# Moving the SwiGLU input tiles of a fused decoder layer by 64 and 32 bytes in SBUF

## The chip, the cores and the metric

The kernel runs on one core of one Trainium2 chip. The metric is the device time of one execution in microseconds (us). All tensors are float32 in DRAM, 256 tokens, model width 1024, SwiGLU width 2816.

## What is computed

One layer of a decoder trunk: a SwiGLU block, a gated mixing part (block-sparse attention beside an RWKV-7 recurrence), a second SwiGLU block, and a final RMSNorm.

```python
def swiglu(h, w_gate, w_up, w_down):
    return (jax.nn.silu(h @ w_gate) * (h @ w_up)) @ w_down

x = x + 0.5 * swiglu(rms_norm(x, norm_ffn1), ffn1_gate, ffn1_up, ffn1_down)   # 1024 -> 2816 -> 1024
h = rms_norm(x, norm_mix)
proj = h @ w_in            # q, k, v of attention; r, k, v of RWKV-7; two gates
y_a = moba_attention(...)  # 8 heads of 64
y_b = rwkv7_time_mix(...)  # 8 heads of 64
merged = sigmoid(ga) * (y_a @ proj_a) + sigmoid(gb) * (y_b @ proj_b)
x = x + merged @ w_out
x = x + 0.5 * swiglu(rms_norm(x, norm_ffn2), ffn2_gate, ffn2_up, ffn2_down)
out = rms_norm(x, norm_final)
```

## The kernel before, in words

**Products in three passes.** Every large product is made in float32r from numbers split into a high and a low part. SP loads a piece of a weight matrix (128 partitions x 8 row blocks x 256 columns, 1 MB) into `w_raw` (line 337, the helper `load`), ScalarE copies it to `w_hi` rounded to float32r (line 560), and VectorE subtracts to get `w_lo` (line 933). There are two buffers of each, used in turn. TensorE then runs the helper `three` (lines 1488 to 1490), which for one 128x128 block of weights issues three matmuls into the same place in PSUM:

```python
mm(dst, whi[slot][:, k_, cols], xl, start=start, stop=False)
mm(dst, wlo[slot][:, k_, cols], xh, start=False, stop=False)
return mm(dst, whi[slot][:, k_, cols], xh, start=False, stop=stop)
```

The second argument is the stationary operand, 128 columns of weights, loaded by an instruction of its own (LDWEIGHTS); the third is the moving operand, 256 columns of the input, one for each token. So each matmul needs a new load of weights, and the load for the next matmul runs while the current one streams its input. The first pieces of a stage issue the same three matmuls through another helper (line 1484).

**The stages.** A SwiGLU block has 22 pieces for gate and up (11 of each, in turn; a piece is 8 row blocks x 2 column blocks x 3 = 48 matmuls) and 12 pieces for down (7, 7 and 8 row blocks for each of 4 groups of 256 columns, so 42, 42 and 48 matmuls). That is 1,056 + 528 = 1,584 matmuls of 256 columns in a block, 3,168 in both. The input of gate and up is `hhi_f`/`hlo_f` (1024 x 256, transposed), that of down is `hid_hi_t`/`hid_lo_t` (2816 x 256), which ScalarE and VectorE write piece by piece from `silu` and `prod`. The mixing part in between uses `hhi_m`/`hlo_m`, `yahi`/`yalo`, `ybhi`/`yblo` and `mhi`/`mlo` as inputs in the same way. In one of its products, the attention values, the roles are exchanged: the weights are the moving operand and `hhi_m`/`hlo_m` the stationary one (lines 1764 to 1766).

**Order.** Each engine has its own program, written out by hand; semaphores order them. TensorE waits for `lo_ready` before each piece, ScalarE for the landed load and for `multiplied` of the piece that used the buffer before.

**Where tiles lie.** SBUF tiles are placed one behind the other within a partition, each beginning at the next multiple of 32 bytes. All six weight buffers are 8,192 bytes per partition, so all begin at the same byte modulo 256, which is 128. The blocks inside them are 1,024 bytes apart, and the two column halves 512 bytes, so every block of weights that is loaded begins at 128 modulo 256. Likewise each block of an input tile begins at the same byte modulo 256 as its tile. `pad_f` is a tile that nothing reads or writes. It stands between `h_f` and `hhi_f`, and `hlo_f`, `silu`, `prod`, `hid_hi_t`, `hid_lo_t`, `out_tok`, `x_tok` and a few small ones follow. The tiles of the mixing part use the same space again at another time, from the place of `h_f` on, and are placed without `pad_f`.

| tile | begins at, modulo 256, before | now | input minus weights, modulo 256, before | now |
|---|---|---|---|---|
| `w_hi`, `w_lo`, `w_raw` | 128 | 128 | | |
| `hhi_f`, `hlo_f` (gate, up) | 64 | 0 | 192 | 128 |
| `hid_hi_t`, `hid_lo_t` (down) | 64 | 32 | 192 | 160 |
| `silu`, `prod` | 64 | 0 | | |
| `out_tok`, `x_tok` | 64 | 32 | | |
| `hhi_m`, `yahi`, `ybhi`, `mhi` and their low parts | 64 | 64 | 192 | 192 |
| attention values: moving `w_hi` (128), stationary `hhi_m` (64) | | | 64 (moving minus stationary) | 64 |

Of the kernel before, what the change touches and what calls it, by code (L numbers as in the profile page):

```python
# [30 lines left out]
P = 128  # L31
# [113 lines left out]
def trunk(nc, A, consts, out):  # L145
    bias_dram = nc.dram_tensor("bias_rows", (H, 16, 384), F32, kind="Internal").ap()
    with ExitStack() as ctx:
        def sb(name, shape, dt=F32, scope=ctx):
            return scope.enter_context(nc.sbuf_tensor(name, shape, dt))
# [45 lines left out]

        with ExitStack() as sc:
            h_f = sb("h_f", [P, KD, T], scope=sc)
            sb("pad_f", [P, 48], scope=sc)
            hhi_f = sb("hhi_f", [P, KD, T], F32R, scope=sc)
            hlo_f = sb("hlo_f", [P, KD, T], F32R, scope=sc)  # L200
            silu = sb("silu", [P, 2, T], scope=sc)
            prod = sb("prod", [P, 2, T], scope=sc)
            hid_hi = sb("hid_hi_t", [P, FT, T], F32R, scope=sc)
            hid_lo = sb("hid_lo_t", [P, FT, T], F32R, scope=sc)
            out_tok = sb("out_tok", [P, 2, D], scope=sc)

            x_tok = sb("x_tok", [P, 2, D], scope=sc)
            raw2 = out_tok[:].rearrange("p a d -> p (a d)").rearrange("p (c w) -> p c w", c=KD)
            vec_rows = sb("vec_rows", [NVEC, P], scope=sc)
            rel = sb("rel", [NB, H], scope=sc)  # L210
            tok = sb("tok", [P, 8], scope=sc)
# [1925 lines left out]
```

## Time and profile before

| | us |
|---|---|
| median of 3 runs | 616.38 |
| the three runs | 616.14, 616.38, 626.31 |
| the profiled execution | 616.02 |
| its span, from first to last instruction | 614.2 |
| TensorE busy (matmul) | 604.6, 98% of the span |
| VectorE busy | 421.3, 69% |
| ScalarE busy | 296.7, 48% |
| GpSimd busy | 101.4, 17% |
| granted TensorE clock, mean | 0.999 of full speed |

A matmul is recorded from its start to its modelled end, 0.28 us, and a new one starts every 0.11 to 0.12 us, so that records overlap and "busy" can't tell how fast matmuls follow each other. The distance between the starts of two matmuls is called the spacing here. In a stretch that is full of matmuls it is (length of the stretch + 0.28 us) / number of records in it, since a record counts when any part of it lies in the stretch. For weight loads (0.19 us) it is reckoned from first start to last.

### The profile page before, as it was taken

How to read it: one execution, taken by the hardware profiler on the slowest of the kernel's cores; microseconds unless marked ns; L12 is line 12 of the kernel's file. 1: busy time of each engine (PE TensorE's matmuls, PEld its weight loads, DVE VectorE, ACT ScalarE, POOL GpSimd, SP SyncE). 2: the span in 40 equal slices, each digit the busy share in tenths (PEclk: the TensorE clock that was granted, in tenths of full speed). 3: DMA queues.
4: the chain of work that ended last, by engine and by line, in shares of the span. 5: the costliest groups of instructions: out<-in, count | busy, mean ns of one | idle time of the engine just before them, and what ended most of it. 6: DMA issues, size and time to landing. Idle time of an engine off the chain costs nothing.

```text
span 614.2 us, 14948 instructions
## 1 busy us (share of the span) xinstructions
PE 604.6 (98%) x6454; PEld 588.8 (96%) x6454; DVE 421.3 (69%) x490; ACT 296.7 (48%) x346; POOL 101.4 (17%) x106
## 2 busy tenths in 40 slices
PE   8999999999999999999999999999999999999996
PEld 8999999999999999989889999999999999999996
DVE  5857787765556369989994447878767676665662
ACT  6734665444434284345655546645544444443341
POOL 1116800000113100023205433004000000000130
PEclk9999999999999999999999999999999999999999
DMA  8677666556556335586342233455656566556541
GB/s 282 224 249 226 205 194 186 182 174 196 184 186 204 108 127 168 191 209 170 99 136 75 73 106 106 137 154 190 202 170 186 195 205 205 186 164 210 174 157 68
DMA packets 100734, 105.37 MB, mean 172 GB/s; under 512 B 2276, under 2 KB 98828, under 8 KB 100692
## 3 DMA queue, kind: packets, MB, share of 16 engines
q1 hardware_dynamic: 99380, 101.47, 51.8%
q0 software_dynamic: 1152, 3.02, 2.1%
q8 instruction: 33, 0.54, 0.4%
q10 hardware_dynamic: 160, 0.27, 0.1%
q14 instruction: 9, 0.07, 0.0%
HBM read 103.50 MB, written 1.25 MB: 171 GB/s over the span
## 4 chain that ended last, share of the span: by engine, by line
PE 85%; DVE 8%; DMA 4%; ACT 3%; issue 0%; SPq 0%; ACTq 0%; DVEq 0%
PE two L1488 25%; PE two L1490 23%; PE two L1489 23%; PE two L1484 11%; DVE w_lo L933 4%; DMA w_raw<-in_ffn_up 2%; ACT w_hi L560 2%; DMA w_raw<-in_ffn_gate 1%; DMA x_tok<-in_x 1%; PE two L1820 1%; DVE w_lo L943 0%; PE two L1764 0%; PE two L1766 0%; PE two L1765 0%; ACT w_hi L572 0%
## 5 line engine op out<-in xcount | busy, mean ns | idle before, releaser
L560 ACT ACTIVATE w_hi<-w_raw 128x2048 fp32r<-128x2048 f32 (+1 forms) x86 | 162.5, 1890 | 240.0 <-PE two L1490 196.0
L933 DVE TENSOR_TENSOR w_lo<-w_raw,w_hi 128x2048 fp32r<-128x2048 f32 (+1 forms) x86 | 200.4, 2330 | 83.5 <-ACT w_hi L560 83.1
L1488 PE MATMUL two<-hlo_f,w_hi 128*128 128x256 f32 x640 | 177.3, 277 | 0.9 <-DVE w_lo L933 0.8
L1489 PE MATMUL two<-hhi_f,w_lo 128*128 128x256 f32 x640 | 176.7, 276 | 0.0
L1490 PE MATMUL two<-hhi_f,w_hi 128*128 128x256 f32 x640 | 176.7, 276 | 0.0
L1488 PEld LDWEIGHTS two<-hlo_f,w_hi 128*128 128x128 f32 x640 | 120.1, 188 | 2.0 <-DVE w_lo L933 1.8
L1489 PEld LDWEIGHTS two<-hhi_f,w_lo 128*128 128x128 f32 x640 | 120.2, 188 | 0.0
L1490 PEld LDWEIGHTS two<-hhi_f,w_hi 128*128 128x128 f32 x640 | 120.1, 188 | 0.0
L1488 PE MATMUL two<-hid_lo_t,w_hi 128*128 128x256 f32 x352 | 97.9, 278 | 0.5
L1490 PE MATMUL two<-hid_hi_t,w_hi 128*128 128x256 f32 x352 | 97.3, 276 | 0.0
L1489 PE MATMUL two<-hid_hi_t,w_lo 128*128 128x256 f32 x352 | 97.3, 276 | 0.0
L1488 PE MATMUL two<-hlo_m,w_hi 128*128 128x256 f32 x288 | 82.7, 287 | 0.9 <-DVE w_lo L933 0.9
L1489 PE MATMUL two<-hhi_m,w_lo 128*128 128x256 f32 x288 | 79.8, 277 | 0.0
L1490 PE MATMUL two<-hhi_m,w_hi 128*128 128x256 f32 x288 | 79.8, 277 | 0.0
L1488 PEld LDWEIGHTS two<-hid_lo_t,w_hi 128*128 128x128 f32 x352 | 66.1, 188 | 1.5 <-DVE w_lo L933 1.3
L1490 PEld LDWEIGHTS two<-hid_hi_t,w_hi 128*128 128x128 f32 x352 | 66.2, 188 | 0.0
L1489 PEld LDWEIGHTS two<-hid_hi_t,w_lo 128*128 128x128 f32 x352 | 66.1, 188 | 0.0
L1488 PEld LDWEIGHTS two<-hlo_m,w_hi 128*128 128x128 f32 x288 | 54.2, 188 | 4.0 <-issue 1.7
L1490 PEld LDWEIGHTS two<-hhi_m,w_hi 128*128 128x128 f32 x288 | 54.1, 188 | 0.0
L1489 PEld LDWEIGHTS two<-hhi_m,w_lo 128*128 128x128 f32 x288 | 54.1, 188 | 0.0
L423 POOL TENSOR_TENSOR sqsum<-x 128x512 f32<-128x512 f32 x3 | 3.1, 1042 | 238.7 <-DVE x L1061 210.3
L1004 DVE TENSOR_TENSOR prod<-two,rstd 128x512 f32<-128x512 f32 x22 | 15.2, 692 | 19.8 <-PE two L1490 19.7
(347 smaller groups left out, 983.8 us busy)
## 6 DMA issues: line engine op xcount, KB each, us to landing
w_raw<-in_ffn_up SPq DMA_DIRECT2D x21, 1024.0 KB, 5.3
w_raw<-in_ffn_gate SPq DMA_DIRECT2D x20, 1024.0 KB, 5.3
w_raw<-in_w_in SPq DMA_DIRECT2D x20, 1024.0 KB, 5.1
w_raw<-in_ffn_down SPq DMA_DIRECT2D x16, 896.0 KB, 4.8
w_raw<-in_ffn_down SPq DMA_DIRECT2D x8, 1024.0 KB, 5.2
w_raw<-in_w_out SPq DMA_DIRECT2D x4, 1024.0 KB, 5.1
w_raw<-in_proj_a SPq DMA_DIRECT2D x4, 512.0 KB, 3.6
w_raw<-in_proj_b SPq DMA_DIRECT2D x4, 512.0 KB, 4.1
```

The costliest lines, as they stand in the source:

```text
L423: nc.gpsimd.tensor_tensor(sqsum[:], pair, pair, ALU.mult).then_inc(sg["sq_sum"], 1)
L560: nc.scalar.activation(whi[slot][:, 0:kts], raw[slot][:, 0:kts], ACT.Copy).then_inc(sg["hi_ready"], 1)
L933: nc.vector.tensor_tensor(wlo[slot][:, 0:kts], raw[slot][:, 0:kts], whi[slot][:, 0:kts].bitcast(F32), ALU.subtract).then_inc(sg["lo_ready" ...
L1004: nc.vector.tensor_tensor(prod[:], bank[1][:].rearrange("p (m t) -> p m t", m=2), rstd2, ALU.mult).then_inc(sg["up_taken"], 1)
L1484: return mm(dst, lhsT, rhs, start=start, stop=True, skip_group_check=True)
L1488: mm(dst, whi[slot][:, k_, cols], xl, start=start, stop=False)
L1489: mm(dst, wlo[slot][:, k_, cols], xh, start=False, stop=False)
L1490: return mm(dst, whi[slot][:, k_, cols], xh, start=False, stop=stop)
L1820: return nc.tensor.transpose(dst[:, at:at + C], src, cst[rows, C_SUI:C_SUI + C])
```

## The change

`pad_f` is 32 in place of 48 floats per partition (128 in place of 192 bytes), and a second unused tile of 8 floats (32 bytes) is put between `prod` and `hid_hi_t`. All tiles from `hhi_f` on begin 64 bytes earlier up to `prod`, and 32 bytes earlier from `hid_hi_t` on. No instruction is added, removed or put elsewhere; only addresses differ.

```diff
             h_f = sb("h_f", [P, KD, T], scope=sc)
-            sb("pad_f", [P, 48], scope=sc)
+            sb("pad_f", [P, 32], scope=sc)
             hhi_f = sb("hhi_f", [P, KD, T], F32R, scope=sc)
             hlo_f = sb("hlo_f", [P, KD, T], F32R, scope=sc)
             silu = sb("silu", [P, 2, T], scope=sc)
             prod = sb("prod", [P, 2, T], scope=sc)
+            sb("pad_hid", [P, 8], scope=sc)
             hid_hi = sb("hid_hi_t", [P, FT, T], F32R, scope=sc)
             hid_lo = sb("hid_lo_t", [P, FT, T], F32R, scope=sc)
             out_tok = sb("out_tok", [P, 2, D], scope=sc)
```

## Rows read from the trace of the kernel before

**Rows 1.** The page: busy time by engine, granted clock, and the chain that ended last.
```profile
PE 604.6 (98%) x6454; PEld 588.8 (96%) x6454; DVE 421.3 (69%) x490; ACT 296.7 (48%) x346; POOL 101.4 (17%) x106
...
PEclk9999999999999999999999999999999999999999
...
PE 85%; DVE 8%; DMA 4%; ACT 3%; issue 0%; SPq 0%; ACTq 0%; DVEq 0%
```

**Rows 2.** The page's groups of SwiGLU matmuls: count, busy us, mean ns.
```profile
L1488 PE MATMUL two<-hlo_f,w_hi 128*128 128x256 f32 x640 | 177.3, 277 | 0.9 <-DVE w_lo L933 0.8
...
L1488 PE MATMUL two<-hid_lo_t,w_hi 128*128 128x256 f32 x352 | 97.9, 278 | 0.5
```

**Rows 3.** Busy time by stretch (columns named in the first row), ten stretches full of matmuls.
```profile
core 0: us, PE busy (x) PEld busy (x) DVE busy (x) ACT busy (x) POOL busy (x), PEclk, DMA share, GB/s
19.60:26.60 7.00, 7.00 (x61) 6.95 (x60) 5.51 (x8) 4.83 (x6) 0.00 (x0) 1.00 0.87 291
51.00:131.00 80.00, 80.00 (x708) 80.00 (x707) 61.49 (x56) 41.07 (x38) 23.07 (x25) 1.00 0.62 196
199.70:213.40 13.70, 13.70 (x119) 13.70 (x117) 4.83 (x7) 2.07 (x3) 2.60 (x6) 1.00 0.38 121
217.00:259.00 42.00, 42.00 (x373) 42.00 (x372) 36.43 (x37) 23.01 (x26) 0.00 (x0) 1.00 0.54 176
269.60:274.90 5.30, 5.30 (x47) 5.30 (x47) 3.23 (x3) 0.94 (x2) 2.77 (x6) 1.00 1.02 151
276.50:281.80 5.30, 5.30 (x47) 5.30 (x47) 4.52 (x4) 0.75 (x1) 5.24 (x3) 1.00 0.86 173
391.00:407.00 16.00, 16.00 (x138) 16.00 (x137) 13.36 (x16) 6.45 (x7) 0.00 (x0) 1.00 0.59 198
419.20:436.20 17.00, 17.00 (x145) 16.95 (x144) 14.29 (x16) 11.63 (x13) 4.30 (x2) 1.00 0.60 186
437.50:580.00 142.50, 142.50 (x1260) 142.50 (x1259) 93.95 (x77) 60.99 (x48) 3.38 (x3) 1.00 0.61 194
596.50:606.50 10.00, 10.00 (x87) 10.00 (x87) 3.07 (x3) 3.14 (x4) 0.75 (x1) 1.00 0.00 0
```

**Rows 4.** Timeline in the down product of the second block: TensorE's matmuls around a wait.
```profile
595.34 0.28 PE L1489 MATMUL two<-hid_hi_t,w_lo 128*128 128x256 f32 x1
595.45 0.28 PE L1490 MATMUL two<-hid_hi_t,w_hi 128*128 128x256 f32 x1
595.85 0.39 PE L1488 MATMUL two<-hid_lo_t,w_hi 128*128 128x256 f32 x1
596.08 0.28 PE L1489 MATMUL two<-hid_hi_t,w_lo 128*128 128x256 f32 x1
596.19 0.28 PE L1490 MATMUL two<-hid_hi_t,w_hi 128*128 128x256 f32 x1
```

**Rows 5.** The weight loads at the same place.
```profile
595.85 0.19 PEld L1488 LDWEIGHTS two<-hid_lo_t,w_hi 128*128 128x128 f32 x1 [0.32 <-DVE w_lo L933]
595.96 0.19 PEld L1489 LDWEIGHTS two<-hid_hi_t,w_lo 128*128 128x128 f32 x1
596.08 0.19 PEld L1490 LDWEIGHTS two<-hid_hi_t,w_hi 128*128 128x128 f32 x1
```

**Rows 6.** Timeline: eight weight loads whose matmuls stream two columns each.
```profile
375.59 0.97 PEld L1484 LDWEIGHTS two<-cst,tmp 128*128 128x128 f32 x8
```

**Rows 7.** Timeline of ScalarE and VectorE for one piece of up, second block.
```profile
502.19 1.92 ACT L560 ACTIVATE w_hi<-w_raw 128x2048 fp32r<-128x2048 f32 x1 [3.00 <-PE two L1490]
504.14 2.29 DVE L933 TENSOR_TENSOR w_lo<-w_raw,w_hi 128x2048 fp32r<-128x2048 f32 x1 [0.54 <-ACT w_hi L560]
507.63 1.92 ACT L560 ACTIVATE w_hi<-w_raw 128x2048 fp32r<-128x2048 f32 x1 [3.00 <-PE two L1490]
```

**Rows 8.** The same two engines for one piece of down, second block.
```profile
575.69 1.71 ACT L560 ACTIVATE w_hi<-w_raw 128x1792 fp32r<-128x1792 f32 x1 [3.73 <-PE two L1490]
577.43 3.00 DVE L933 TENSOR_TENSOR w_lo<-w_raw,w_hi 128x1792 fp32r<-128x1792 f32 x1
```

**Rows 9.** What the weight loads waited for: us in total, times, longest.
```profile
PEld two L1488 <- DVE w_lo L933: 4.2, 7, 1.1
```

## The prediction

> **What bounds the kernel now.** I read the page first. TensorE is busy 98% of the span at full granted clock, and the chain that ended last is TensorE for 85% of its length [rows 1]. VectorE (69%) and ScalarE (48%) come next, so the time is how fast matmuls follow each other. The counts say whose matmuls they are: 3 x (640 + 352) of the two SwiGLU blocks in the loops [rows 2], to which line 1484 adds 3 x 64, 3,168 together, as the program has it. At 113 to 118 ns each that is about 360 of the 616 us. The change touches only where the inputs of these lie.
>
> "Busy" can't show a spacing, so I took stretches that are full of matmuls of 256 columns and divided. There are two spacings, and hardly anything between them [rows 3]. **The short one**: (142.5 + 0.28) / 1260 = 113.3 ns from 437.5 to 580 us, (80 + 0.28) / 708 = 113.4 from 51 to 131, (42 + 0.28) / 373 = 113.4 in the mixing part from 217 to 259. **The long one**: the stretches from 199.7, 269.6, 276.5, 391 and 596.5 have (13.7 + 5.3 + 5.3 + 16 + 10 + 5 x 0.28) / (119 + 47 + 47 + 138 + 87) = 51.7 / 438 = 118.0 ns. The clock is 1.00 in all of them. Both occur with the same input distance of 192 bytes: the down product has the short one up to 580 and the long one after 596.5. The timeline shows where it went over: TensorE waited for `w_lo`, started again at 595.85, and stayed at the long spacing [rows 4]. So the spacing is a way of running into which the engine falls at a restart and in which it stays until the next one. The reader should see in rows 3 that 142.5 us went by without a change.
>
> What is there besides the 113.3 ns? With matmuls that stream only two columns, eight weight loads follow each other at (0.97 - 0.19) / 7 = 111.4 ns [rows 6]. So loading 128 columns of weights takes nearly the whole of the short spacing, and streaming 256 columns of input beside it adds 1.9 ns in the short way and 6.6 ns in the long way. Those few ns are all that a better place of the tiles can be seen to save, and the rows give no ceiling for what a worse place costs.
>
> **The change part by part.**
> *Gate and up, 192 to 128 bytes (2,112 matmuls), and down, 192 to 160 (1,056).* No row shows either distance. The nearest are on both sides: 192 in nearly all rows, and 64 for the attention values, where the weights are the moving operand; their two stretches (269.6 and 276.5) have (10.6 + 0.56) / 94 = 118.7 ns, the long spacing within the error of such a division, and no worse [rows 3]. 128 and 160 lie between the two. I take the spacing of 192, as the nearer row for 160 and as near as the other for 128, and because it holds for most of the stretches: cost 0. The bounds: from below, all SwiGLU matmuls at the bare weight load. About 250 of them have the long spacing now (61 from 19.6, some 100 of the 145 from 419.2, the rest being the output projection, and 87 from 596.5), and 2,900 the short. That is 2,900 x 1.9 ns + 250 x 6.6 ns = 5.5 + 1.7 = 7.2 us less. The first two loads after the restart are 0.11 us apart, 595.85 and 595.96 [rows 5], which by its rounding allows 110 ns or less: 2,900 x 3.3 + 250 x 8 ns = 11.6 us less as the far end. From above, the nearest row is the long spacing for all: 2,900 x 4.7 ns = 13.6 us more. The farthest row is the restart itself, where a matmul follows the load of its own weights without overlap, 596.08 - 595.85 = 0.23 us [rows 4]: over 300 us more, if loads and streams could not run together at all. As they have run together at both distances on either side, I leave that end out of the range.
>
> *What a faster TensorE would meet.* ScalarE starts `w_hi` when TensorE leaves the buffer (502.19), VectorE has `w_lo` at 504.14 + 2.29 = 506.43, and TensorE turns to that piece about when ScalarE starts the next, 507.63 [rows 7]: 1.2 us to spare, against at most 48 x 3.3 ns = 0.16 us that a piece could become shorter. In the down product 575.69 to 577.43 + 3.00 = 580.43 is 4.74 us, beside 42 x 113.3 ns = 4.76 us of matmuls [rows 8]. Nothing is to spare there when GpSimd slows VectorE, so such a gain would partly turn into waits; they are 4.2 us in seven waits now [rows 9].
>
> *The other tiles.* `silu`, `prod`, `out_tok` and `x_tok` begin at other bytes too. VectorE and ScalarE read and write them, inside the 1.2 us above: cost 0. Without that cover it would be 22 pieces by whatever an instruction got longer, of which no row tells. The transposes of `x_tok` are 16 at the start.
>
> *More or fewer restarts in the long way.* If all SwiGLU matmuls ran at the short spacing, 250 x 4.7 ns = 1.2 us would be saved.
>
> The sum is 0 against the profiled execution, 616.02 us (span 614.2 and 1.8 around it). The median of the runs, 616.38, is 0.4 above. I forecast 616.0. What a measurement of this kernel can tell from no change is about 2%, or 12.3 us here: below 604.1 or above 628.7.
>
> A rule speaks against any effect at all. The Trainium skill, "SBUF — State Buffer", section "Who interferes with whom", gives TensorE two SBUF read ports, one for the moving operand and one for the weight loads, independent of each other, and says that it never waits for anyone. By that rule an address changes nothing and the time is 616.0. The trace agrees only in part: 111.4 ns for a load with little beside it, 113.3 or 118.0 with a stream beside it, so that something is shared or in step between the two.
>
> **The rivals.**
> 1. *The stream stops costing anything.* The 1.9 and 6.6 ns above the bare load are collisions of the two reads, and the new distances avoid them. For it: two spacings for one and the same work look like two orders in which such reads can fall. Against: the short spacing was the same to 0.1 ns in three products, which looks like a fixed price. Time 616.0 - 7.2 = 608.8, with 604.4 as the far end; over 2% only if even the 110 ns is beaten and no wait takes it back.
> 2. *The restarts fall the other way.* At the new distances most restarts end in the long spacing. For it: both stretches at distance 64 are long, and the long one is seen at every kind of input. It needs only that the two restarts ahead of the long loops end so. Time 616.0 + 13.6 = 629.6 if all do. If the one loop of 1,260 does it is 5.9 more, 621.9. The third of the runs shown, 626.31, may have been such a case: 10 us / 4.7 ns is some 2,100 matmuls, but no trace of it exists.
> 3. *The other side: a third, longer spacing.* The order of the two reads at 128 or 160 bytes is a worse one than any seen. The place is every matmul of the loops, the price one more step of the same 4.7 ns: 2,900 x 9.4 + 250 x 4.7 ns = 28.4 us, 644.4. It decides as soon as the mean spacing of SwiGLU matmuls rises by 12.3 us / 3,150 = 3.9 ns, from 113.7 to 117.6 ns, so the long spacing everywhere is just enough. For it: nothing covers a slower matmul in a kernel with TensorE at 98%. Against: distances on both sides have at most 118 to 119 ns.
> 4. *The change doesn't do what it says.* The addresses follow from tile sizes, so only a misreading of what counts (another modulus than 256) could make it so. It ends at 616.0 and belongs to the forecast.
>
> **How the numbers follow.** Forecast, with rival 4: 0.43, between 614.8 and 617.5. Rival 1: 0.18, from 604.4 to 612, of which 0.05 beyond 2%. Rival 2: 0.22, from 618 to 629.6, of which 0.04 above 628.7. Rival 3: 0.17, all of it above. This makes 0.05 faster, 0.21 slower and 0.74 within 2%. The range leaves out half of rival 1's lower part and most of rival 3: 607 to 632. The predicted time is the forecast's own, 616.0.
>
> **What the profile of the changed kernel would show.** Counts as before. For the forecast, 113.3 ns from 437.5 to 580 and from 51 to 131, and the mixing part, whose tiles haven't moved, with 113.4 from 217 to 259 in any case. For rival 1, about 1,280 records in the same 142.5 us and a down product with more than 4.2 us of waits. For rival 2, 118 ns in whole loops and 113 in others. For rival 3, a spacing above 119 ns. If gate and up differ from down, the distance decides and not the restart. I am wrong if the spacing in the loops is neither 113.3 nor 118.0, or if VectorE's instructions on `prod` and `hid_lo_t` get so much longer that the 1.2 us are used up.

## The result, and the profile after

The changed kernel takes 629.97 us (median of 4 executions, 629.09 to 630.40), the kernel before 618.18 in the same comparison (4 executions, 616.14 to 626.31). The ratio is 1.0197, 95% interval 1.0157 to 1.0236: slower, clear of noise, but whether by the 2% that counts as a difference here stays open. Ratios in this document leave out slow executions, those more than 1.5% above the fastest of their kernel: here the one of 626.31, and in e2 one of 628.70. My forecast was 616.0 and no change. A second comparison, told below, gives 1.0177 (1.0130 to 1.0223). Over all comparisons the kernel before was run 31 times, with a median of 620.7 and a spread from 615.75 to 626.31. The 616.02 of the profiled execution, against which the prediction was summed up, lies at the lower end of that.

The page of the kernel after (lines are one higher, since the edit adds one):

```profile
PE 620.1 (99%) x6454; PEld 604.8 (96%) x6454; DVE 421.6 (67%) x490; ACT 296.4 (47%) x346; POOL 101.8 (16%) x106
...
PEclk9999999999999999999999999999999999999999
...
PE 93%; DVE 4%; DMA 1%; ACT 1%; issue 0%; SPq 0%; DVEq 0%; ACTq 0%
...
L1489 PE MATMUL two<-hlo_f,w_hi 128*128 128x256 f32 x640 | 180.7, 282 | 0.0
...
L1489 PE MATMUL two<-hid_lo_t,w_hi 128*128 128x256 f32 x352 | 99.3, 282 | 0.0
```

Counts, VectorE, ScalarE and GpSimd are as before [rows 1, 2]. The waits for `w_lo` went down [rows 9], since TensorE is the slower one now:

```profile
PEld two L1489 <- DVE w_lo L934: 1.9, 5, 1.1
```

Busy time by stretch, with the columns of [rows 3]:

```profile
51.00:131.00 80.00, 80.00 (x676) 80.00 (x676) 59.28 (x55) 38.71 (x36) 23.56 (x25) 1.00 0.59 185
149.00:173.50 24.50, 24.50 (x209) 24.50 (x208) 12.76 (x11) 9.37 (x9) 3.38 (x3) 1.00 0.61 199
225.00:267.00 42.00, 42.00 (x373) 42.00 (x372) 36.39 (x38) 22.73 (x25) 0.00 (x0) 1.00 0.54 176
416.00:426.00 10.00, 10.00 (x91) 10.00 (x90) 6.79 (x6) 5.21 (x6) 3.37 (x3) 1.00 0.66 211
445.00:557.00 112.00, 112.00 (x947) 112.00 (x946) 71.84 (x59) 48.09 (x40) 0.00 (x0) 1.00 0.59 185
559.00:593.50 34.50, 34.50 (x297) 34.50 (x296) 21.35 (x18) 12.65 (x8) 3.37 (x3) 1.00 0.59 195
```

The reader should divide as in [rows 3]. Gate and up, in both blocks: (80.28 + 112.28) / (676 + 947) = 118.6 ns, where 113.3 stood. Down: 24.78 / 209 = 118.6 and 34.78 / 297 = 117.1. The mixing part, whose tiles did not move: 42.28 / 373 = 113.4, the same 373 records in 42 us as before.

The sum, against the profiled execution before: 2,112 x (118.6 - 113.7) = 10.3 us, 1,056 x (117.9 - 113.7) = 4.4 us, less 2.3 us of waits for `w_lo`. That is 12.4. (117.9 is the mean over all 1,056 matmuls of down, some at 117.3 and some at 118.7 ns, from their start times in the trace.) The spans differ by 628.6 - 614.2 = 14.4. Nearly all of the other 2.0 us, 1.9, was lost before the first matmul of gate, and not by the change. The timeline of TensorE there, before:

```profile
5.58 1.10 PE L1622 MATMUL two<-cst,x_tok 128*128 128x128 f32 x8 [0.22 <-DMA x_tok<-in_x]
6.97 1.09 PE L1622 MATMUL two<-cst,x_tok 128*128 128x128 f32 x8 [0.29 <-DMA x_tok<-in_x]
...
9.09 0.36 PE L1484 MATMUL two<-hlo_f,w_hi 128*128 128x256 f32 x1
```

and after:

```profile
6.02 3.67 PE L1623 MATMUL two<-cst,x_tok 128*128 128x128 f32 x16 [0.67 <-DMA x_tok<-in_x]
...
10.97 0.36 PE L1485 MATMUL two<-hlo_f,w_hi 128*128 128x256 f32 x1
```

The transposes follow each other at 0.21 us, nearly twice the 0.11 of before. I read this as the lower of TensorE's two clock levels. The column PEclk can't confirm it, since it says 1.00 where nothing is recorded: the trace's record of the granted clock begins only at 5.59 us in the execution before and at 10.42 in the one after. But each of these is the place at which the spacing falls from 0.21 to 0.11. The kernel before, run again (e16), shows the same 0.21 for its first eight, and its record begins at 6.84 us, so this differs from one execution to the next.

### The profile page after: what moved, and what is told of

Its sections match the earlier page's. It is cut to its first block, busy times and chain, and to the rows that moved or that the text cites. A ratio compares the mean times of both kernels' runs of the same rounds, so it can differ in the third digit from the quotient of the medians.

```text
span 628.6 us, 14948 instructions
## 1 busy us (share of the span) xinstructions
PE 620.1 (99%) x6454; PEld 604.8 (96%) x6454; DVE 421.6 (67%) x490; ACT 296.4 (47%) x346; POOL 101.8 (16%) x106
## 4 chain that ended last, share of the span: by engine, by line
PE 93%; DVE 4%; DMA 1%; ACT 1%; issue 0%; SPq 0%; DVEq 0%; ACTq 0%
PE two L1489 26%; PE two L1490 25%; PE two L1491 25%; PE two L1485 14%; DVE w_lo L934 2%; DMA x_tok<-in_x 1%; PE two L1821 1%; PE two L1623 1%; PE two L1765 0%; ACT w_hi L561 0%; PE two L1767 0%; PE two L1766 0%; DVE lg L1165 0%; PE two L2095 0%; DVE stat L1170 0%
## 5 line engine op out<-in xcount | busy, mean ns | idle before, releaser
L1489 PE MATMUL two<-hlo_f,w_hi 128*128 128x256 f32 x640 | 180.7, 282 | 0.0
L1490 PE MATMUL two<-hhi_f,w_lo 128*128 128x256 f32 x640 | 180.4, 282 | 0.0
L1491 PE MATMUL two<-hhi_f,w_hi 128*128 128x256 f32 x640 | 180.3, 282 | 0.0
L1489 PE MATMUL two<-hid_lo_t,w_hi 128*128 128x256 f32 x352 | 99.3, 282 | 0.0
L1490 PE MATMUL two<-hid_hi_t,w_lo 128*128 128x256 f32 x352 | 98.7, 281 | 0.0
L1491 PE MATMUL two<-hid_hi_t,w_hi 128*128 128x256 f32 x352 | 98.7, 280 | 0.0
```

## The experiments

Theory D: the distance between an input tile and the weights, modulo 256 bytes, sets the spacing of each product. Theory R: the restarts fell the long way by chance. Theory O: other tiles (`silu`, `prod`) made VectorE slower. Every time in this section is that of the profiled execution unless a median is named. The mixing part stayed at 192 in every run but e3, e4 and e13, and by the start times in the traces its stretches had 113.3 or 117.8 ns each time, on four chips, so that it serves as a control.

**e1, gate and up alone at 128**

```diff
-            sb("pad_f", [P, 48], scope=sc)
+            sb("pad_f", [P, 32], scope=sc)
+            sb("pad_hid", [P, 16], scope=sc)      # before hid_hi_t
```

> Gate and up at a distance of 128 bytes, down back at 192, everything else as in the changed kernel but out_tok and x_tok. Theory D (the distance between input and weights, modulo 256, sets the spacing of each product by itself): 118.7 ns in the gate and up loops, all the way and in both blocks, and 113.3 or 118.0 in down as before. 2,112 matmuls x 5 ns = 10.5 us above before, about 627. Theory R (the restarts fell the long way by chance): 113.3 in some loops, 118.0 in others, and a time that changes from run to run by 5 us or more. Theory O (other tiles moved, silu and prod above all, and slower VectorE work is what costs): VectorE's instructions get longer and matmuls wait for w_lo, while the spacing inside a piece stays at 113.3.

Median 627.39 us, ratio to before 1.011 (1.0037 to 1.0183). Busy time by stretch: gate and up, down, and gate and up of the second block:

```profile
45.00:135.00 90.00, 90.00 (x761) 90.00 (x760) 64.67 (x59) 43.56 (x40) 24.30 (x26) 1.00 0.62 194
139.00:172.00 33.00, 33.00 (x294) 33.00 (x293) 18.54 (x15) 13.69 (x12) 3.38 (x3) 1.00 0.62 200
445.00:553.00 108.00, 108.00 (x912) 108.00 (x912) 68.42 (x58) 46.27 (x38) 0.00 (x0) 1.00 0.59 185
```

90.28 / 761 = 118.6 and 108.28 / 912 = 118.7 in gate and up, 33.28 / 294 = 113.2 in down. Theory D, in both blocks. The medians differ by 6.4 us; the 10.5 that I expected lies within the interval, which reaches to 11.4.

**e2, down alone at 160**

```diff
+            sb("pad_hid", [P, 56], scope=sc)      # before hid_hi_t
```

> Gate and up as before at 192, down alone at 160 bytes. silu and prod are where they were before. Theory D: 113.3 ns in the gate and up loops, 117.3 to 118.7 in down, 1,056 x 4.3 ns = 4.5 us above before, about 620 to 621. Theory R: no difference from before beyond its own spread. Theory O, with silu and prod unmoved: 616 to 617.

Median 624.57 us of 10, ratio 1.0039 (0.9998 to 1.0080): by time alone this is open, and 624.57 lies above the 620 to 621 that I expected. The trace decides it. First gate and up, then down, then the mixing part:

```profile
445.00:548.00 103.00, 103.00 (x912) 103.00 (x911) 68.06 (x58) 46.32 (x38) 0.00 (x0) 1.00 0.62 194
552.00:585.00 33.00, 33.00 (x284) 33.00 (x283) 19.93 (x16) 11.69 (x8) 3.38 (x3) 1.00 0.60 197
```
```profile
220.00:262.00 42.00, 42.00 (x359) 42.00 (x358) 35.49 (x37) 21.99 (x23) 0.00 (x0) 1.00 0.55 176
```

103.28 / 912 = 113.2 ns in gate and up, 33.28 / 284 = 117.2 in down. The mixing loop at 192, which nobody moved, ran at 42.28 / 359 = 117.8 in this execution, where it has 113.4 otherwise. So theory R is also true of distance 192, and adds a spread of its own.

**e3, the weights moved and no input; e4, weights and SwiGLU inputs moved together**

```diff
+        sb("pad_w", [P, 16])                      # before w_raw, both
-        idle = sb("idle", [P, 74])
+        idle = sb("idle", [P, 58])
-            sb("pad_f", [P, 48], scope=sc)        # e4 only
+            sb("pad_f", [P, 64], scope=sc)        # e4 only
```

> The weight buffers begin 64 bytes later and no input tile of a product is moved: every distance is 128 in place of 192, in the mixing part too. Theory D: 118.7 ns in all loops, also in the mixing part from about 217 to 259 us, where the changed kernel had kept 113.3; 3,168 x 5 ns + 1,300 x 3 ns = 20 us above before, about 636. If the place of the input alone counts (its own address modulo 256): 113.3 as before and 616 to 620. Theory O: as before.

> Weights and the SwiGLU inputs both 64 bytes later: the SwiGLU distances stay at 192 at another absolute place, the mixing part is at 128. Theory D: 113.3 ns in the SwiGLU loops, with 118.0 after some restarts, and 118.7 in the mixing loops; about 620 to 626. If the absolute place of input or weights counts: another spacing than 113.3 and 118.0 in the SwiGLU loops.

633.15 and 624.56 us. e3, gate and up, then the mixing loop:

```profile
45.00:135.00 90.00, 90.00 (x760) 90.00 (x760) 65.85 (x59) 43.58 (x40) 24.31 (x26) 1.00 0.61 190
225.00:268.00 43.00, 43.00 (x365) 43.00 (x364) 36.19 (x38) 21.89 (x23) 0.00 (x0) 1.00 0.54 172
```

e4, gate and up of the first block, the mixing loop, gate and up and down of the second block:

```profile
45.00:130.00 85.00, 85.00 (x752) 85.00 (x751) 64.84 (x59) 43.59 (x40) 23.80 (x26) 1.00 0.64 201
220.00:261.00 41.00, 41.00 (x348) 41.00 (x347) 35.53 (x36) 20.52 (x19) 0.00 (x0) 1.00 0.56 180
442.00:552.00 110.00, 110.00 (x937) 110.00 (x936) 71.09 (x58) 46.84 (x40) 0.00 (x0) 1.00 0.59 188
591.00:604.00 13.00, 13.00 (x117) 13.00 (x116) 8.92 (x7) 3.91 (x3) 3.40 (x3) 1.00 0.66 216
```

e3 has 118.8 and 118.6 ns everywhere, with every input tile, `silu` and `prod` where they were: theory O and the place of the input alone are out. (`x`, `rstd` and other tiles between the weights and `idle` moved along, but they did in e4 too, which kept the short way.) The time is 3 us under the 636 that I expected. e4 has 113.4 in the first block, 118.6 in the mixing part, whose distance became 128, and 110.28 / 937 = 117.7, then 113.5, in the second block. The distance decides, not the place. At 192 there are two ways, at 128 one.

**e5 to e8, four more distances, each in both products**

```diff
-            sb("pad_f", [P, 48], scope=sc)
+            sb("pad_f", [P, 16], scope=sc)        # e5: no such line; e6: 16; e7: 56; e8: 24
+            sb("pad_hid", [P, 48], scope=sc)      # e5: 16; e6: 48; e7: 32; e8: 32
```

> Gate and up at a distance of 0 (no padding), down at 64. Theory D1 (the two reads collide, and the nearer they begin the more it costs): 0 is the worst distance, over 118.7 ns in gate and up, over 630 us; down at 64 like 192 seen from the other side, so 113.3 or 117.8. Theory D2 (no such order; 192 is the one distance with a short way): 0 and 64 both 117 to 119 ns at every restart, about 631.

> Gate and up at 64, down at 0. Theory D1: gate and up 113.3 or 117.8, down over 118.7; 622 to 632. Theory D2: 117 to 119 ns in both, about 631. In both theories the spacing belongs to the distance, so gate and up must show here what down shows at 64, and down what gate and up show at 0.

> Gate and up at 224, down at 96. Theory D1: 224 is nearer to 0 than 192 and costs more than it, 118 ns or more; 96 lies between 64 and 128, 117 to 119. About 630. Theory D2: 117 to 119 ns in both. If 224 keeps the short way (113.3), neither the distance from 0 nor the one special place is the rule.

> Gate and up at 96, down at 224: the distances of the run before, exchanged between the products. The spacing found at 96 and at 224 there must come back here in the other product if distance alone decides; if it belongs to the product, 113.3 or 118 ns stays with the same product. About 625 to 631.

630.69, 630.16, 630.10 and 631.02 us. e5, gate and up at 0, down at 64:

```profile
445.00:557.00 112.00, 112.00 (x936) 112.00 (x935) 70.88 (x58) 47.09 (x40) 0.00 (x0) 1.00 0.58 184
560.00:594.00 34.00, 34.00 (x291) 34.00 (x290) 20.78 (x17) 11.97 (x8) 3.38 (x3) 1.00 0.59 191
```

e6, gate and up at 64 in two stretches, down at 0:

```profile
28.10:38.30 10.20, 10.20 (x92) 10.20 (x91) 5.43 (x6) 4.07 (x4) 0.92 (x2) 1.00 0.90 258
...
446.00:556.00 110.00, 110.00 (x936) 110.00 (x936) 71.17 (x58) 46.69 (x39) 0.00 (x0) 1.00 0.59 187
558.00:593.00 35.00, 35.00 (x294) 35.00 (x294) 21.17 (x18) 12.45 (x8) 3.37 (x3) 1.00 0.59 192
```

e7, gate and up at 224, down at 96:

```profile
445.00:556.00 111.00, 111.00 (x940) 111.00 (x939) 71.24 (x58) 47.17 (x40) 0.00 (x0) 1.00 0.59 186
558.00:593.00 35.00, 35.00 (x294) 35.00 (x293) 21.19 (x17) 12.41 (x8) 3.38 (x3) 1.00 0.59 191
```

e8, gate and up at 96, down at 224:

```profile
445.00:558.00 113.00, 113.00 (x944) 113.00 (x943) 71.24 (x58) 47.28 (x40) 0.00 (x0) 1.00 0.57 183
560.00:594.00 34.00, 34.00 (x290) 34.00 (x289) 20.64 (x17) 12.07 (x8) 3.38 (x3) 1.00 0.58 191
```

At 0: 112.28 / 936 = 120.0 and 35.28 / 294 = 120.0. At 96: 113.28 / 944 = 120.0 and 35.28 / 294 = 120.0. At 224: 111.28 / 940 = 118.4 and 34.28 / 290 = 118.2. At 64: 110.28 / 936 = 117.8 and 34.28 / 291 = 117.8, and once, in the first stretch of e6, 10.48 / 92 = 113.9, which the start times make 113.3. Each spacing came back in the other product. D1 falls: 96 costs as much as 0 and lies between 64 and 128, which cost less, so there is no order by nearness. D2 falls too: it gave 0 at most 119 ns, and the short way to 192 alone.

**e9 and e10, the distances exchanged, and the last of the eight**

```diff
-            sb("pad_f", [P, 48], scope=sc)
+            sb("pad_f", [P, 40], scope=sc)        # e9: 40; e10: 8
+            sb("pad_hid", [P, 56], scope=sc)      # e9: 56; e10: no such line
```

> The distances of the changed kernel exchanged: gate and up at 160, down at 128. Theory D: down 118.7 ns throughout, gate and up 117.3 or 118.7 by restart, about 628 to 631. Theory P (the spacing belongs to the product, whatever the distance): gate and up 118.7, down 117.3 or 118.7, as in the changed kernel.

> Both at 32, the last of the eight distances that tiles can have. By the order of the others (0 and 96 at 120.0, 224 at 118.3, 160 at 117.3 or 118.7, 64 and 192 with a short way at 113.3): if 32 mirrors 224 as 64 mirrors 192, 118.3 ns; if it is only near to 0, 120.0. No short way in either: 629 to 635 us.

629.54 and 627.68 us. e9, gate and up at 160 in both blocks, down at 128:

```profile
30.00:136.00 106.00, 106.00 (x896) 106.00 (x895) 75.98 (x67) 49.98 (x46) 25.57 (x28) 1.00 0.63 198
...
446.00:556.00 110.00, 110.00 (x939) 110.00 (x939) 71.07 (x58) 47.30 (x40) 0.00 (x0) 1.00 0.60 188
559.00:593.00 34.00, 34.00 (x288) 34.00 (x288) 20.63 (x16) 11.63 (x8) 3.36 (x3) 1.00 0.58 189
```

e10, gate and up at 32 in both blocks:

```profile
32.00:136.00 104.00, 104.00 (x894) 104.00 (x893) 75.31 (x67) 48.53 (x44) 25.29 (x28) 1.00 0.63 199
...
444.00:555.00 111.00, 111.00 (x944) 111.00 (x944) 71.29 (x59) 47.55 (x40) 0.00 (x0) 1.00 0.60 187
```

160 has two ways, 106.28 / 896 = 118.6 and 110.28 / 939 = 117.4; 128 has 34.28 / 288 = 119.0, by the start times 118.7 again; theory P, that the spacing belongs to the product, is out. 32 has two, 104.28 / 894 = 116.6 and 111.28 / 944 = 117.9. Neither guess about 32 was right, and its time lies below the 629 to 635 that I expected.

**e11, 256 bytes further; e15, 16 bytes to either side of 192**

```diff
-            sb("pad_f", [P, 48], scope=sc)
+            sb("pad_f", [P, 112], scope=sc)       # e11
+            def late(name, k, by):                # e15, for hhi_f, hlo_f, hid_hi_t, hid_lo_t
+                t = sb(name, [P, k * T + 8], F32R, scope=sc)
+                return t[:, by:by + k * T].rearrange("p (k t) -> p k t", t=T)
...                                                # e15: pads before each of them set to fit
+            hhi_f = late("hhi_f", KD, 4)          # 4 floats, 16 bytes
```

> Padding of 112 in place of 48 floats: all SwiGLU tiles 256 bytes later, distances modulo 256 as before. Theory D with modulus 256: only 113.3 and 117.8 ns in the SwiGLU loops, 616 to 626. With a modulus of 512 or more another spacing would come, as it did for each move by 32 or 64 bytes.

> 16 bytes to either side of 192: gate and up at 176, down at 208, by views that begin 16 bytes into tiles at 160 and 192. If the short way lasts over a width of more than 16 bytes, 113.3 ns in one or both. If it hangs on 192 (and 64) alone, 117 to 119 in both, about 630. A finding of only 113.3 at all restarts of one of them would be a way to a faster kernel.

617.25 and 631.08 us. e11, gate and up and most of down in the second block:

```profile
440.00:580.00 140.00, 140.00 (x1237) 140.00 (x1237) 91.81 (x76) 60.12 (x48) 3.20 (x3) 1.00 0.62 196
```

e15, down at 208 in two stretches, gate and up at 176:

```profile
149.00:173.00 24.00, 24.00 (x204) 24.00 (x203) 12.58 (x11) 8.62 (x8) 3.38 (x3) 1.00 0.63 200
175.00:189.00 14.00, 14.00 (x123) 14.00 (x122) 7.43 (x5) 5.36 (x5) 2.34 (x2) 1.00 0.64 206
446.00:558.00 112.00, 112.00 (x941) 112.00 (x941) 71.24 (x58) 46.87 (x40) 0.00 (x0) 1.00 0.58 184
```

140.28 / 1237 = 113.4 in e11: the same distance modulo 256 behaves alike. 176 has 112.28 / 941 = 119.3, 208 has 24.28 / 204 = 119.0 and 14.28 / 123 = 116.1, by the start times 119.2 and 116.6. The short way is gone 16 bytes to either side.

**e12, e13 and e14, one tile of the three passes moved**

```diff
+            sb("pad_lo", [P, 48], scope=sc)       # e12: hlo_f at 128; e14: 32 floats, hlo_f at 64
+        sb("pad_w", [P, 16])                      # e13: before w_lo, w_lo at 128 from the inputs
```

> Only hlo_f is moved, to 128 from the weights; hhi_f and down stay at 192. Of three matmuls one streams from the moved tile: (hlo_f, w_hi), (hhi_f, w_lo), (hhi_f, w_hi). Theory N (a stream collides with the load of the next matmul's weights, here w_lo) and theory S (a stream collides with what was loaded for it, here w_hi) both give a spacing other than 113.3 and 118.7. They part in the next run. If one of three streams at 128 spoils nothing, gate and up stay at 113.3 or 117.8.

> Only w_lo is moved, to 128 from hhi_f, hid and the mixing inputs; w_hi stays at 192. Theory N: the load of w_lo runs beside the stream of hlo_f, at 128 as in the run before, and the other two pairs are at 192 as there, so gate and up show the very spacing of the run before, to 0.1 ns. Theory S: the pair (hhi_f, w_lo) is at 128, another place in the three than before, with w_lo's matmul the long one. If the tiles of one matmul and of the next both count, the two runs differ.

> hhi_f stays at 192, hlo_f is at 64, the other distance at which the short way has been seen; down at 192. If a stream needs only a good distance of its own: 113.3 or 117.8 in gate and up, like before. If the tiles of neighbouring matmuls have to fit as well, as the runs with only hlo_f or only w_lo at 128 leave open: a spacing of its own, 116 to 119.

627.83, 631.62 and 626.08 us. Gate and up of the second block in e12:

```profile
445.00:557.00 112.00, 112.00 (x946) 112.00 (x945) 71.33 (x59) 47.48 (x40) 0.00 (x0) 1.00 0.58 185
```

in e13:

```profile
447.00:558.00 111.00, 111.00 (x941) 111.00 (x941) 71.23 (x59) 47.59 (x40) 0.00 (x0) 1.00 0.60 187
```

and in e14:

```profile
443.00:553.00 110.00, 110.00 (x937) 110.00 (x936) 71.00 (x58) 46.96 (x40) 0.00 (x0) 1.00 0.59 188
```

118.7, 118.3 and 117.7 ns. One tile of three off 192 is enough to lose the short way. Theory N wanted the same spacing in e12 and e13 to 0.1 ns; they differ by 0.4, over more than 900 matmuls each, and no stretch of 40 or more in gate and up of e12 is under 118.7 by its start times, where e13 has 118.2 in all but its first. Theory S isn't shown by that: which pair collides stays open. In e14, with one stream at 64 and two at 192, gate and up had the long way at every start, as 64 nearly always has.

**e16, the kernel before again, and e17, the changed kernel again** (only the unused tile renamed)

> The kernel before once more, only the unused tile renamed. Theory R for its spread: the time is 614.8 plus 4.45 ns for each SwiGLU matmul that ran at 117.8, so that time and trace must agree: a run of 616 has some 250 to 300 of them, one of 620 about 1,200, one of 625 about 2,300. If the time differs and the spacings don't, its spread has another cause.

> The changed kernel once more, against more executions of the kernel before. By the theory of two ways the kernel before lies anywhere from 615 to 627 us, with its median near 620, and the changed one within 627 to 631, since 128 has one spacing and the two of 160 differ by 1.3 ns x 1,056 = 1.4 us. The ratio should come out at 1.013 to 1.018, less than the 1.020 of the first comparison. If the changed kernel spreads as widely as the kernel before, the account of the spread by distance 192 is wrong.

e16 took 618.54 us. Its loops are like those of [rows 3], but the last piece of down in the first block had the long way:

```profile
186.00:195.00 9.00, 9.00 (x78) 9.00 (x78) 4.92 (x3) 2.45 (x2) 0.00 (x0) 1.00 0.71 231
```

(The division gives 119.0 for this short stretch, the start times 117.8.) Counted matmul by matmul, 1,131 of all its 256-column matmuls ran at the long spacing, against 953 in the execution of before: 178 x 4.4 ns = 0.8 us of the 2.5 us between the spans. 1.0 us more is the later rise of the clock at the start, and 1.0 us more lies in its waits (0.3 us came back elsewhere). My expectation put the whole spread down to the SwiGLU matmuls at 117.8: for 618.54 it wanted (618.54 - 614.8) us / 4.45 ns = 840 of them, and the trace has some 400. So the two ways are one cause of the spread and not the only one. No execution of before that took 625 us was profiled; e4 had 1,300 matmuls of one block in a row in the long way, which at 4.5 ns each is an estimated 6 us.

e17: median 630.47 us (6 executions, 628.03 to 632.31), before in the same comparison 620.16 (11, 615.75 to 622.78), ratio 1.0177 (1.0130 to 1.0223). The changed kernel spreads over 4.3 us and the one before over 7.0. 632.31 lies above the 631 that I expected.

## Why the prediction was wrong, point by point

- *What bounds the kernel, and the two spacings.* Right. The time is the spacing of TensorE's matmuls, and it went up by what the spacing went up by. That a restart chooses the way is right for 192. From the start times in all traces I took every stretch of 20 or more matmuls of one product without a gap of over 0.15 us between two starts, and its mean spacing from the ninth matmul on: at 192, 226 of 321 were short; at 64, 1 of 46; at 0, 32, 96, 128, 160 and 224, none of 145. No stretch of 45 or more at 192 changed its way; two were disturbed for a few matmuls and fell back into the short one.
- *"No row shows either distance. The nearest are on both sides ... 128 and 160 lie between the two. I take the spacing of 192."* This is the step that failed. It took the spacing to change evenly between two distances. It doesn't: 64 and 192 have a short way and 96, 128 and 160 between them have none. The term of 0 is 10.3 us for gate and up and 4.4 us for down, by the sum above; e1 and e2 show both apart. The rows of 64 had a warning that I priced as harmless: both stretches were long [rows 3], although 192 was mostly short.
- *The upper bound, "the long spacing for all: 13.6 us more".* As a size it was nearly right, 629.6 against 629.97, and by chance. Rival 2 gave it to chance restarts at the new distances, but at 128 no stretch went any other way (none of 71 outside 118.4 to 118.9 ns).
- *Rival 3, a third, longer spacing.* Right in kind, with a chance of 0.17, and wrong in price: 118.6 ns is a spacing of its own, but 5.3 ns above the short one and not 9.4. The worst mean seen anywhere is 120.0.
- *Rival 1, a stream that costs nothing beside the load.* No distance of the ten did that; 113.3 is the least seen.
- *The other tiles cost 0.* Right (e3). *Waits for w_lo shrink when TensorE slows.* Not in the prediction, 2.3 us.
- *"I am wrong if the spacing in the loops is neither 113.3 nor 118.0", and "If gate and up differ from down, the distance decides".* Both signs were good: gate and up had 118.6, down in part 117.3, and e1 to e4 bore out the distance.
- *The base.* I summed against one execution of 616.02 and three times, one of which was 626.31. The median of 31 is 620.7, that of the ten of the changed kernel 630.2. With that the change costs 9.5 us, 1.5% (the two comparisons by themselves give 2.0% and 1.8%), and the forecast would have been a few us too low for no change at all.
- The rule of the Trainium skill that I weighed ("SBUF — State Buffer", "Who interferes with whom": two independent read ports in TensorE, no waiting) would have given 616.0. Here the measurement decides against it as a rule for the spacing: with the same instructions, an address modulo 256 moves it between 113.3 and 120.0 ns. Whether the two reads wait for each other isn't shown by that.

No version beats the kernel before. All distances that are multiples of 32 bytes were run, with two more around 192. 192 is the best, and 64 has the same short way but seldom falls into it.

## What to carry to other kernels

Where matmuls with a weight load each fill TensorE, the distance between the moving tile and the weights, modulo 256 bytes, is worth up to 6% of their time, and it can't be interpolated: measure each distance. Read the spacing, start to start, and not the busy time, and look whether it keeps one value from one restart to the next. Where there are two, one execution is no base: take the median of many before a sum is made against it.

## What the runs showed of the hardware

Spacing of 256-column float32r matmuls with a load of 128 columns each, by distance (input minus weights, modulo 256 bytes), at full granted clock. The means are those of the start times, from the ninth matmul of a stretch on; the divisions above agree with them to 0.3 ns in long stretches:

| distance | 0 | 32 | 64 | 96 | 128 | 160 | 176 | 192 | 208 | 224 |
|---|---|---|---|---|---|---|---|---|---|---|
| ns | 120.0 | 116.7 or 117.9 | 113.3 (seldom) or 117.8 | 120.0 | 118.7 | 117.3 or 118.7 | 119.3 | 113.3 or 117.8 | 116.6 or 119.2 | 118.3 |

At the upper of the two clock levels, 2.4 GHz, the least is 113.3 x 2.4 = 272 periods and the most 120.0 x 2.4 = 288. The single spacings behind a mean differ in kind. In the short way of 192 nearly all are 113 or 114 ns, and at 0 nearly all are 120. At 128 they repeat over five matmuls, as about 115, 118, 121, 120 and 119 ns, and at 96 they run from 115 to 125 for the same mean of 120.0. So a mean between the two ends isn't a mixture of matmuls at 113.3 and at 120.0. Which of the two reads waits, if one does, wasn't tried. The way of running also outlasts the end of one product and the start of the next, as long as TensorE doesn't have to wait: from 437.5 to 580 us over 1,260 matmuls [rows 3].
